# VectorE in place of GpSimd for the low halves of the heads' weights and the samples' key products

## The reference

```python
proj = h @ w_in_odd[j]
q, k, v = jnp.split(proj, 3, axis=-1)
...
k_past = cache_k[j, page_table].reshape(Bn, n_past, C_HEADS, 2, C_HEAD_DIM).astype(k.dtype)
...
s = jnp.einsum('bqhcd,bkhcd->bhcqk', q, k).astype(jnp.float32)
dist = (q_pos[:, None] - k_pos[None, :]).astype(jnp.float32)
s = s - slopes[None, :, None, None, None] * dist
s = jnp.where(dist >= 0, s, -jnp.inf)
p = jax.nn.softmax(s, axis=-1)
w = p[:, :, 0] - lam * p[:, :, 1]
return jnp.einsum('bhqk,bkhe->bqhe', w.astype(v.dtype), v)
```

## Time and profile before

| | |
|---|---|
| median of 3 runs | 3059.59 us (3058.96 to 3062.16) |
| the profiled execution, its own time | 3064.17 us |
| its span | 3062.3 us |
| PE busy | 2877.0 us, 94% of the span |
| DVE busy | 1539.4 us, 50% |
| ACT busy | 1033.4 us, 34% |
| GpSimd busy | 586.7 us, 19% |
| mean granted clock of TensorE | 0.97 |

### The profile page before, as it was taken

How to read it: one execution, slowest core, us unless ns; L and a number is a source line. 1 busy time by engine, 2 the same in 40 slices (tenths; PEclk the granted TensorE clock), 3 DMA queues, 4 the chain that set the end, 5 groups by cost and what they waited for, 6 DMA issues and landing times. The chain is left out here.

```text
span 3062.3 us, 46088 instructions
## 1 busy us (share of the span) xinstructions
PE 2877.0 (94%) x18504; PEld 2759.3 (90%) x18504; DVE 1539.4 (50%) x2300; ACT 1033.4 (34%) x1747; POOL 586.7 (19%) x322
## 2 busy tenths in 40 slices
PE   6999988979999999999998999996899999999997
PEld 5999988859899999999988888885889999999996
DVE  3057434356744444444481576773565443444436
ACT  3325534435511111111162566662462111111114
POOL 1221135300122222222100122210003222222220
PEclk8999989969999999999999999997999999999999
DMA  4111100033321111111141222213431111111103
GB/s 146 48 42 36 30 9 0 1 104 105 105 71 41 41 41 41 41 55 41 29 139 38 69 78 77 69 57 127 133 106 46 55 50 55 41 41 41 41 14 113
DMA packets 183498, 185.01 MB, mean 60 GB/s; under 512 B 10469, under 2 KB 168549, under 8 KB 183296
## 3 DMA queue, kind: packets, MB, share of 16 engines
q1 hardware_dynamic: 183380, 183.45, 19.3%
HBM read 151.13 MB, written 32.57 MB: 60 GB/s over the span
## 5 line engine op out<-in xcount | busy, mean ns | idle before, releaser
L1541 DVE TENSOR_TENSOR acc<-acc,ps 128x1032 f32<-128x1032 f32 x144 | 177.0, 1229 | 231.9 <-PE ps L124 231.9
L1945 PE MATMUL ps<-mix_in0hi,in0wh 128*128 128x344 f32 x600 | 197.6, 329 | 14.9 <-POOL mix_in0lo L244 9.1
L124 PE MATMUL ps<-midlo,rest0wh 128*128 128x344 f32 x984 | 209.1, 321 | 0.0
L124 PE MATMUL ps<-mix_out1lo,rest1wh 128*128 128x344 f32 x984 | 209.0, 321 | 0.0
L124 PE MATMUL ps<-midhi,rest0wl 128*128 128x344 f32 x984 | 208.6, 320 | 0.0
L124 PE MATMUL ps<-mix_out1hi,rest1wh 128*128 128x344 f32 x984 | 208.5, 320 | 0.0
L124 PE MATMUL ps<-midhi,rest0wh 128*128 128x344 f32 x984 | 208.5, 320 | 0.0
L124 PE MATMUL ps<-mix_out1hi,rest1wl 128*128 128x344 f32 x984 | 208.5, 320 | 0.0
L1945 PE MATMUL ps<-mix_in0lo,in0wh 128*128 128x344 f32 x600 | 192.8, 321 | 0.0
L1945 PE MATMUL ps<-mix_in0hi,in0wl 128*128 128x344 f32 x600 | 192.8, 321 | 0.0
L124 PEld LDWEIGHTS ps<-midhi,rest0wl 128*128 128x128 f32 x984 | 165.6, 188 | 0.0
(11 more groups left out here) (507 smaller groups left out, 7024.2 us busy)
## 6 DMA issues: line engine op xcount, KB each, us to landing
wraw<-in_w_ffn_gate SPq DMA_DIRECT2D x22, 1024.0 KB, 5.4
wraw<-in_w_ffn_up SPq DMA_DIRECT2D x22, 1024.0 KB, 5.3
wraw<-in_w_ffn_down SPq DMA_DIRECT2D x22, 1024.0 KB, 4.8
wraw<-x_scratch SPq DMA_DIRECT2D x96, 172.0 KB, 2.9
x_scratch<-acc SPq DMA_DIRECT2D x72, 172.0 KB, 3.1
wraw<-in_w_in_even SPq DMA_DIRECT2D x24, 512.0 KB, 3.9
wraw<-in_w_in_odd SPq DMA_DIRECT2D x24, 512.0 KB, 4.7
sr_page<-in_cache_k SPq DMA_DIRECT2D x16, 512.0 KB, 4.2
```

The costliest lines, as they stand in the source:

```text
L124: ins = pe.matmul(ps[:, 3 * r + c, 0:CH], w, h[:, c * CH:(c + 1) * CH], start=first and n == 0, stop=last and n == 2)
L1541: dve.tensor_tensor(a, a, region(T.ps, m % 2), ALU.add).then_inc(collected, 1)
L1945: ins = pe.matmul(bank(n, c), w[n % 2][:, k, :], cut(h[:, k, :], c), start=first and m == 0, stop=final and m == 2)
```

## The change

GpSimd's two large operations of the stage go to DVE. `SampleRows.vector` now multiplies the page and then sums it, both at i = 3 and i = 6. `lo_weights` becomes a function of DVE, called for the next head's values at the end of i = 2, and for the keys of the head after that at the end of i = 7; at the start of the stage DVE makes both low halves of head 0, and that of head 1's keys behind the three `move_k` of head 0. On ACT, the high half of head 1's keys is made ahead of the split of head 0's queries and keys. GpSimd keeps the small copies alone.

```diff
-    def gpsimd(self, pool, b, j):
-        pool.wait_ge(self.query_in, 16 * b + 16)
-        pool.wait_ge(self.page_in, 16 * (PAGES * b + j) + 16)
-        pool.tensor_tensor(self.page[:], self.page[:], self.query[:], ALU.mult).then_inc(self.multiplied, 1)
-
     def vector(self, dve, b, j):
+        dve.wait_ge(self.query_in, 16 * b + 16)
+        dve.wait_ge(self.page_in, 16 * (PAGES * b + j) + 16)
+        dve.tensor_tensor(self.page[:], self.page[:], self.query[:], ALU.mult).then_inc(self.multiplied, 1)
         dve.wait_ge(self.multiplied, PAGES * b + j + 1)
...
+                    hi_weights(0, 1)
                     act.wait_ge(par_in, 64)
                     act.wait_ge(k_moved, 3)
                     for n in range(2):
                         split_hi(0, 0, n)
-                    hi_weights(0, 1)
...
             def _(dve):
+                def lo_weights(b, g):
+                    dve.wait_ge(w_hi[b], g + 1)
+                    if not (isinstance(g, int) and g == 0):
+                        dve.wait_ge(unit_made, UNITS * (g - 1) + 3 * b + 3)
+                    dve.tensor_tensor(slot_l[b][:], raw[b], slot_h[b][:], ALU.subtract).then_inc(w_lo[b], 1)
+
...
+                        if i == 2 and more:
+                            lo_weights(1, h + 1)
+                        if i == 7 and more2:
+                            lo_weights(0, h + 2)
                         if i in (3, 6):
                             samples.vector(dve, h, i // 3 - 1)
...
                     own = Steps(dve, lam_own)
+                    for b in range(2):
+                        lo_weights(b, 0)
...
                         move_k(0, c)
+                    lo_weights(0, 1)
...
                     if not first:
                         keep(1, h)
-                    samples.gpsimd(pool, h, 0)
                     if more:
-                        lo_weights(1, h + 1)
                         keep(0, h + 1)
-                    samples.gpsimd(pool, h, 1)
-                    if more2:
-                        lo_weights(0, h + 2)
```

More of the change, by code:

```diff
@@ L3281, in _ @@
             def _(pool):
[L3282 to L3286, removed]
                 def keep(b, g):
@@ L3295, in head @@
                         keep(1, h)
-                    samples.gpsimd(pool, h, 0)
                     if more:
-                        lo_weights(1, h + 1)
                         keep(0, h + 1)
-                    samples.gpsimd(pool, h, 1)
-                    if more2:
-                        lo_weights(0, h + 2)
                 def start():
-                    for b in range(2):
-                        lo_weights(b, 0)
                     keep(0, 0)
-                    lo_weights(0, 1)
                     keep(1, 0)
```

## The result

| | before | changed | ratio, 95% interval |
|---|---|---|---|
| median of 20 runs each | 3059.94 us (3057.26 to 3063.27) | 3064.62 us (3063.06 to 3067.18) | 1.0016 [1.0009, 1.0022] |
| the profiled execution | 3064.17 us, span 3062.3 | 3063.49 us, span 3061.7 | |

A forecast was written before the change was run, and what follows sets the result against it. PE bounds the kernel, busy 94% of the span, so moved work counts only where PE waits. Terms sum to +8.3 us, +4.4 with the clock; 3064.17 + 4.4 - 4.58 = 3064.0 us, range 3056 to 3070.

The forecast's parts named there:

- The two waits: New PE waits for DVE: third `move_k` in heads 0 to 6, +8.4 us; keys' low half at five head starts, +4.85.
- The signs that were named: About 1.2 and 1 us at the new waits, head stretch some 51, first wait near 8.0, last two tiles' clock 1.00.
- The product: Page product at i = 3, ahead of the third `move_k`: 1.2 us in each of seven heads, +8.4.
- The low half: Keys' low half at the end of i = 7, awaited by PE: 0.97 us in each of five heads, +4.85.
- Start, first tile, last head's waits: Stage start -1.1 us, negated maximum of the first tile no longer held -1.05, weighting awaited in the last head -1.9.
- More comes back at ACT's gap and the first tiles: Rival, chance 0.13: head 4's ACT wait returns 2 to 4 us, first tiles' clock 3.2; 3057.6 to 3061.0 us.
- The split's -0.9: Split at i = 4: six heads give back some of PE's wait for the weighting, 0 to 1.3 us, taken as -0.9.
- The clock's -3.9: Last head: with its 3.20 us wait shrunk, TensorE keeps full clock behind it, half of 7.97 busy us, -3.9.
- The carried 4.58 us: Profiled execution of the kernel before over the median of its runs, subtracted from the forecast total: 4.58 us.
- The rival that the low clock stays: Last head keeps TensorE's low clock, so the new waits stand unpaid: +8.3, 3067.9 us; chance 0.33.
- DVE is ahead: Rival, chance 0.08: DVE, no longer held, is ahead at both new waits, so neither comes: -8.85, 3050.7 us.

The follow-up runs named there:

- e1: Changed kernel with the first page's product and sum moved from the end of i = 3 to i = 4, ahead of the splits; 3058.58 us, 0.9992 of before.
- e3: Changed kernel with the first page's work moved to i = 4 and the keys' low half ahead of i = 7's maxima; 3059.2 us, 0.9994 of before.
- e7: Kernel before with SP's head-start loads waiting for ACT's last move of values and DVE's first weighting; 3079.39 us, 1.0062 of before.
- e9: Changed kernel with the pages' products back on GpSimd, the low halves staying on DVE; 3064.24 us, 1.0011 of before.
- e0: Kernel before, unchanged, run again for a second trace; 3057.56 us (one run), stage 3.32 us shorter than in the first trace.
- e5: e3 with the last head's two page products and sums moved to where DVE stands idle; 3055.49 us, 0.9987 of before.
- e6: e5 with SP's head-start loads also waiting for ACT's last move of values and DVE's first weighting; 3051.49 us, 0.9974 of before.
- e8: Kernel before with only the pages' products on DVE, in the places the change gives them; 3069.11 us, 1.0031 of before.
- e10: e6 with heads 2 to 5 written out instead of a loop; 3051.94 us, 0.9970 of before.

## Why the prediction was right, and what in it was not

**The two waits** were right in place, kind and count, and settled by e1 to e3: both vanish when the work stands elsewhere. The signs that were named came too: 1.18 us for `move_k` and 0.84 for the low half in head 2, a stretch of 51.30 us, a first wait of 7.84 and a granted clock of 1.00 in the last two tiles. The product cost 9.20 instead of 8.4, as the sum of the page starts 1.35 us behind the product's start (1826.43, 1827.78), not 1.2: it waits for the product's end. The low half cost 5.21 instead of 4.85.

**Start, first tile, last head's waits** were right to half a microsecond. DVE, free of GpSimd, shows 0.22 and 0.23 for the small operations throughout.

**"More comes back at ACT's gap and the first tiles"** was given 0.13, and in the pair of traces both came: -2.29 and -1.45. Leaving them at zero in the sum is the step that failed. Its time (3057.6 to 3061.0) did not come, as the other terms cost more than the sum had; nor do its own figures give it, since 2 to 4 us and 3.2 are 5.2 to 7.2 together, not 3 to 6.4. "If they were what held ACT, 2 to 4 us return": e7 shows that, with 1.97 us where the two traces of before have 4.39 and 3.62. For the first tiles the cause is open. The low clock there lasted 6.9 and 6.8 us in the two traces of before and 3.4 or 3.5 in every other run, also in e9, where PE waited 3.74 us ahead of it as before. So the shorter wait is not needed to get it back.

**The split's -0.9** was not there (-0.1). With the low half and the page in its new places, the split starts when ACT's high half is done, and the weighting behind it ends as late as before.

**The clock's -3.9** measured -3.57 in the last two tiles of this pair, but 1.3 of it came in e0 too, without the change. By these traces 2.3 to 3.6 us belong to the change, and over the whole last head, waits and clock together, 2.5 to 5.0 against the 5.8 forecast; the runs don't settle it closer. One reading behind it was thin: the 12.40 us at 1.00 are followed at once by a granted clock of 0.51, from 2070.70 to 2074.20 in the trace of before. In the changed kernel the low stretch there is 6.9 us long, not 3.5, so a part of the low clock came earlier and did not go.

**The carried 4.58 us** supposed that what the profiled execution had over the median lay outside the change. In e0 2.99 us lay ahead of the stage and 3.32 within, in the very places (ACT's gap, the clock) that the change then shortened. So the sum's errors cancel: the terms were 3.1 us too low together, the two returns 3.7 too high, and that the total came within 0.6 us of the median is partly luck. The rival that the low clock stays (0.33) did not come, with 1.00 in the last two tiles, but its price was less certain than the sum made it.

**The rival "DVE is ahead"** got 0.08, rightly as the change stands. The Trainium skill's rule beside it ("GPSIMD Engine Reference", "4.1 Engine selection") is right on the duration, 1.22 against 2.34 us. Once the work lies in idle time, the same operations on DVE make the kernel 4.8 us faster than before (e5), and 8.8 with the loads held back as well (e6).

## What to carry to other kernels

Work that leaves a slow engine costs where it is put: find the queue's idle time (here 2.61, 1.02 and 4.37 us) and place each piece there, ahead of a wait that is already paid, not ahead of an instruction that the bounding engine awaits. When one wait goes, look for the next instruction on the same queue that the waiting engine needs. Before costing against a single profiled execution, take a second trace: what differs between two runs of one kernel (here 3.3 us in the stage) is no term of a change.

## What the runs showed of the hardware

- Some operations of GpSimd and DVE exclude each other for the whole instruction, in both directions: a DVE operation of 0.23 us took 2.23 beside a GpSimd product of 2.40 (e7); in the changed kernel GpSimd's copy of 0.19 us took 0.95 to 0.97 beside DVE's low half (1753.54 and 1855.78). Others pass: beside GpSimd's low half of 3.03 us in head 2 of before, DVE's `move_k` out of PSUM took its usual 0.51, and in e8 the page's sum took its usual 1.22 beside the low half that then held the weighting. The Trainium skill, "SBUF — State Buffer", section "SBUF: two separate sides", calls the port pair that the two share an exclusive lock, held for the whole instruction; the rows of the held operations agree. What it costs depends on what lies beside it: 19 us in e7, for loads that start some 3 us later.
- Behind a loop's return an engine can stand still for microseconds with no releaser in the profile ("issue"): ACT 2.1 to 4.6 us, DVE 3.0 to 6.7 in the versions with the longer loop body. The longest stops are those where SP's loads began ahead of them; written out (e10), there is none. Packets of instructions move at the return (three of 8 KB in before, seven in e6); that they are what the engine waits for is likely and not shown.
- The low clock behind nearly the same wait (3.20 and 3.11 us) of one kernel lasted 10 us in one execution and 6.8 in the next.
